# Finishing a gated recurrence tile by tile, making weights' low parts half a unit later, and loading an activation table earlier, in a three-mixer float32 transformer on one Trainium2 core

## The chip, the cores and the metric

The kernel runs on one core of one Trainium2 chip. The metric is the device time in microseconds of one execution, as the median of several runs; lower is better. Device time holds the span of the profile (first to last instruction) and a little around it.

## The reference, cut to what matters

The model takes 512 tokens of width 1024, kept in float32, through seven stages:

1. a gated FFN (SiLU gate, width 2816), a gated linear attention mixer, and another FFN;
2. an FFN, a differential attention mixer, and another FFN;
3. the third mixer, `hybrid_layer`, which ends the model.

The third mixer is what the change touches most. It projects the normalised input to six streams. Two of them, `xl` and `gl`, feed a recurrence, and four (`q`, `k`, `v`, `ga`) feed an attention of 8 heads:

```python
    xl = causal_depthwise_conv(xl, conv_w, conv_b)
    # rg_lru:
    r = sigmoid(xg @ w_a + b_a);  i = sigmoid(xg @ w_i + b_i)
    log_a = -LRU_C * r * softplus(-lam)
    a = exp(log_a)
    mult = sqrt(-expm1(2.0 * log_a));  mult[first token] = 1.0
    bterm = mult * (i * xb)
    h[t] = a[t] * h[t-1] + bterm[t]        # along the 512 tokens
    y_lru = h * silu(gl)
    y_att = attention(rms(q), rms(k), v) * silu(ga)
    out = x + gate * (concat(y_lru, y_att) @ w_out)
```

Every stage begins with an RMS norm, so it needs `rsqrt(mean(x*x) + eps)`, which this kernel makes from a logarithm and an exponential.

## The kernel before, in words

**Layout and matmuls.** All activations are held transposed, as tiles of 128 channels x 512 tokens. Every large matmul is made with float32 precision out of three faster ones: weights and activations are each split into a high part (`whi`, `xh`) and a low part (`wlo`, `xl`), and `rows` (line 1606) adds hi x hi, hi x lo and lo x hi. The weights come in panels (SyncE's queue loads them into four `raw` buffers, line 579) that are cut into units of 128 output channels. A unit is 8 x 3 = 24 matmuls of 512 columns. Unit numbers below are written as n; a unit's parts live in one of NSLOT = 4 slots, so unit n + 3's parts can be made once TensorE is done with unit n - 1.

**Who makes the parts.** ScalarE makes `whi` of a unit by a copy (`w_hi`, line 614), VectorE makes `wlo` as `raw - whi` (`w_lo`, line 1029) and waits for `whi`. SyncE may refill a `raw` buffer when VectorE has made the last `wlo` of its panel (`lo_done`, in `load`, line 575).

**Order of work.** Each engine runs its instructions in program order and waits on semaphores. For the mixers the order is a list of steps, written by hand for differential attention (`diff_steps`, line 182) and by a planner with due times for the third mixer (`hybrid_steps`, line 262). All engines walk the same list. A unit is issued as two steps, `("half", tag, i, 0)` and `("half", tag, i, 1)`, each 12 matmuls, and other steps stand between: `attend n` (scores of query block n, its row maximum on VectorE, its exponential on ScalarE), `comb n` (VectorE divides by the sum), `turn n` (TensorE transposes the block, ScalarE copies it out of PSUM), `pv`, `vT`, `ss` (sum of squares for the norm of q or k), `qk` (that norm applied on VectorE, ScalarE copies k's halves), `gmm`/`gadd` (gates of the recurrence), `lru p` (piece p of the recurrence), and the gate and output steps. A due time counts half-steps: `(15, ("lru", 5))` puts piece 5 beside the 15th half.

In the third mixer the units follow as xl0 to xl3, q0, k0, v0, q1, gate 4, k1, v1, q2, k2, v2, gate 0, q3, k3, v3, and five more gates. The block `attend 0` stands before the first half of k1. Around the change the list of before reads:

```
half q1 0, lru 1, qk k0, vT 0, half q1 1, done q1, lru 2, half gate4 0, lru 3, ss q1, half gate4 1, done gate4, qk q1,
attend 0, half k1 0, gmin 4, attend 1, comb 0, gexp 4, half k1 1, done k1, lru 4, gate 4,
attend 2, comb 1, half v1 0, ss k1, turn 0, attend 3, comb 2, half v1 1, done v1, lru 5, qk k1, turn 1,
attend 4, comb 3, half q2 0, vT 1, turn 2, attend 5, comb 4, half q2 1, done q2, lru 6, turn 3,
attend 6, comb 5, half k2 0, ss q2, pv 0, turn 4, attend 7, comb 6, half k2 1, done k2, qk q2, turn 5,
attend 8, comb 7, half v2 0, ss k2, turn 6, attend 9, comb 8, half v2 1, done v2, qk k2, turn 7,
attend 10, comb 9, half gate0 0, vT 2, pv 1, ya 0, ...
```

**When TensorE waits in it.** `attend n` needs the row maximum of `attend n-2` (two PSUM banks). `turn n` needs `comb n` and ScalarE's copy of `turn n-1` (one bank). `ss` needs ScalarE's square of that projection. A unit's first half needs the bank of the unit three before to have been read.

**The recurrence** (lines 973 to 1000 on ScalarE, 1519 to 1543 on VectorE). Its four tiles of channels stand side by side in `rg` (the decay a), `ig` (i * xb), `th` (the square root) and `xc` (the convolution's result, then h). Pieces 0 to 3 make a and the argument of the square root. Piece 4 on ScalarE is one exponential over 2048 columns (the square root as exp of half a logarithm). Piece 5 on VectorE is one memset for the first token, one multiplication over 2048 columns and the scans of tiles 0 and 1, piece 6 the scans of tiles 2 and 3.

**Tables.** ScalarE's functions lie in tables. `act` (line 596) loads the one with logarithm and exponential at the first Exp or Ln after a Silu, Sigmoid or Tanh (line 599); the loads in the other direction are put in by the compiler and show under line 604. In an FFN the last Silu comes at the last gate tile of part 1; the next Ln is that of the following stage's norm (`norm_factor`, line 637). In the third mixer TensorE can't begin before this norm is done; in the differential one the first sum of squares of k waits for it.

## Time and profile before

| | us |
|---|---|
| median of 3 runs | 2320.44 (2319.05 to 2321.05) |
| the profiled execution | 2316.55 |
| its span | 2314.8 |
| TensorE busy | 2252.8 (97%) |
| VectorE busy | 1270.2 (55%) |
| ScalarE busy | 907.0 (39%) |
| GpSimd busy | 154.0 (7%) |
| mean granted clock of TensorE | 0.992 |

The profiled execution took 3.9 us less than the median; its span lies 1.75 us under its own time. Busy time is the time in which an engine has an instruction under way; idle time of an engine that isn't on the path to the end costs nothing. "PEclk" is the clock that TensorE was granted: 1.00 is 2.4 GHz, 0.50 is 1.2 GHz.

### The profile page before, as it was taken

How to read it: one execution, taken by the hardware profiler on the slowest of the kernel's cores; microseconds unless marked ns; L12 is line 12 of the kernel's file. 1: busy time of each engine (PE TensorE's matmuls, PEld its weight loads, DVE VectorE, ACT ScalarE, POOL GpSimd, SP SyncE). 2: the span in 40 equal slices, each digit the busy share in tenths (PEclk: the TensorE clock that was granted, in tenths of full speed). 3: DMA queues.
4: the chain of work that ended last, by engine and by line, in shares of the span. 5: the costliest groups of instructions: out<-in, count | busy, mean ns of one | idle time of the engine just before them, and what ended most of it. 6: DMA issues, size and time to landing. Idle time of an engine off the chain costs nothing.

```text
span 2314.8 us, 24688 instructions
## 1 busy us (share of the span) xinstructions
PE 2252.8 (97%) x9842; PEld 1798.7 (78%) x9842; DVE 1270.2 (55%) x1964; ACT 907.0 (39%) x1399; POOL 154.0 (7%) x127
## 2 busy tenths in 40 slices
PE   7999999899899999999999999999999999999999
PEld 6888887676677888888888887777688888876677
DVE  6443445877755434454433446777566536546663
ACT  4222223555433222233322325777442222237562
POOL 2000012000040000020000021000220000110000
PEclk9999999999999999999999999999999999999999
DMA  5323224021124232133223223222144334232210
GB/s 186 101 82 109 96 69 148 19 92 55 37 75 157 86 123 91 64 118 109 86 97 109 78 87 107 71 71 89 55 136 146 118 118 141 87 114 64 74 55 37
DMA packets 201747, 217.39 MB, mean 94 GB/s; under 512 B 4969, under 2 KB 194537, under 8 KB 201633
## 3 DMA queue, kind: packets, MB, share of 16 engines
q1 hardware_dynamic: 194960, 193.48, 25.8%
q0 software_dynamic: 6528, 22.26, 2.8%
q8 instruction: 79, 1.29, 0.2%
q14 instruction: 36, 0.29, 0.0%
q10 hardware_dynamic: 144, 0.08, 0.0%
HBM read 213.66 MB, written 6.32 MB: 95 GB/s over the span
## 4 chain that ended last, share of the span: by engine, by line
PE 88%; DVE 7%; ACT 3%; issue 2%; DMA 0%; SPq 0%; DVEq 0%; ACTq 0%
PE ps L1573 86%; PE ps L1577 1%; DVE sb_wlo L1037 1%; ACT sb_whi L604 1%; DVE sb_gla_at L1289 1%; DVE sb_gla_ek L1274 1%; DMA sb_raw<-ffn_w_gu 0%; ACT sb_xh L604 0%; DVE sb_gla_eq L1277 0%; DVE sb_xl L1042 0%; DVE sb_gla_xb L1269 0%; ACT sb_hyb_rg L604 0%; DVE sb_dif_p L1344 0%; DVE sb_gla_d L1256 0%; ACT sb_dif_k L604 0%
## 5 line engine op out<-in xcount | busy, mean ns | idle before, releaser
L1573 PE MATMUL ps<-sb_xh,sb_whi 128*128 128x512 f32 x2120 | 849.0, 400 | 24.0 <-DVE sb_xl L1042 10.1
L1573 PE MATMUL ps<-sb_xh,sb_wlo 128*128 128x512 f32 x2120 | 831.3, 392 | 0.0
L1573 PE MATMUL ps<-sb_xl,sb_whi 128*128 128x512 f32 x2120 | 830.9, 392 | 0.0
L1037 DVE TENSOR_TENSOR sb_wlo<-sb_raw,sb_whi 128x1024 fp32r<-128x1024 f32 (+2 forms) x401 | 475.1, 1189 | 554.6 <-ACT sb_whi L604 553.3
L604 ACT ACTIVATE sb_whi<-sb_raw 128x1024 fp32r<-128x1024 f32 (+2 forms) x401 | 387.1, 968 | 601.2 <-PE ps L1573 592.9
L1573 PEld LDWEIGHTS ps<-sb_xh,sb_whi 128*128 128x128 f32 x2120 | 402.1, 190 | 118.8 <-issue 26.4
L1573 PEld LDWEIGHTS ps<-sb_xl,sb_whi 128*128 128x128 f32 x2120 | 401.8, 190 | 86.9 <-issue 6.0
L1573 PEld LDWEIGHTS ps<-sb_xh,sb_wlo 128*128 128x128 f32 x2120 | 401.1, 189 | 86.0
L1573 PE MATMUL ps<-sb_ffn_ah,sb_whi 128*128 128x512 f32 x704 | 277.6, 394 | 0.0
L1573 PE MATMUL ps<-sb_ffn_ah,sb_wlo 128*128 128x512 f32 x704 | 276.0, 392 | 0.0
L1573 PE MATMUL ps<-sb_ffn_al,sb_whi 128*128 128x512 f32 x704 | 273.3, 388 | 0.0
L1066 DVE TENSOR_TENSOR sb_ffn_u<-ps,sb_rb 128x512 f32<-128x512 f32 x88 | 60.7, 690 | 179.1 <-PE ps L1573 179.1
L1573 PEld LDWEIGHTS ps<-sb_ffn_ah,sb_wlo 128*128 128x128 f32 x704 | 132.1, 188 | 30.9
L1573 PEld LDWEIGHTS ps<-sb_ffn_al,sb_whi 128*128 128x128 f32 x704 | 132.2, 188 | 29.4
L604 ACT ACTIVATE sb_ffn_ah<-sb_ffn_u 128x512 fp32r<-128x512 f32 x88 | 55.6, 632 | 252.1 <-DVE sb_ffn_u L1072 252.1
L1573 PEld LDWEIGHTS ps<-sb_ffn_ah,sb_whi 128*128 128x128 f32 x704 | 132.4, 188 | 26.3
L604 ACT ACTIVATE sb_ffn_g<-sb_ffn_g 128x512 f32<-128x512 f32 x88 | 55.6, 632 | 167.4 <-DVE sb_ffn_g L1063 167.3
L1075 DVE TENSOR_TENSOR sb_ffn_al<-sb_ffn_u,sb_ffn_ah 128x512 fp32r<-128x512 f32 x88 | 61.0, 693 | 61.4 <-ACT sb_ffn_ah L604 61.4
L2012 POOL TENSOR_TENSOR sb_sqs<-sb_xT 128x512 f32<-128x512 f32 x7 | 9.2, 1311 | 1254.9 <-DVE sb_xT L1101 900.5
L1063 DVE TENSOR_TENSOR sb_ffn_g<-ps,sb_rb 128x512 f32<-128x512 f32 x88 | 60.2, 684 | 25.2 <-ACT sb_rb L604 25.2
L2018 POOL TENSOR_TENSOR sb_sqs<-sb_sqs,sb_sq 128x512 f32<-128x512 f32 x44 | 71.8, 1632 | 3.4
L1072 DVE TENSOR_TENSOR sb_ffn_u<-sb_ffn_u,sb_ffn_g 128x512 f32<-128x512 f32 x88 | 60.9, 692 | 11.1 <-ACT sb_ffn_g L604 2.4
(249 smaller groups left out, 1774.6 us busy)
## 6 DMA issues: line engine op xcount, KB each, us to landing
sb_raw<-ffn_w_gu SPq DMA_DIRECT2D x86, 1024.0 KB, 5.2
sb_raw<-ffn_w_down SPq DMA_DIRECT2D x32, 1024.0 KB, 4.9
sb_raw<-gla_w_in SPq DMA_DIRECT2D x12, 1024.0 KB, 5.4
sb_raw<-diff_w_in SPq DMA_DIRECT2D x12, 1024.0 KB, 5.2
sb_ada_raw<-w_ada POOLq DMA_DIRECT2D x12, 1024.0 KB, 6.3
sb_raw<-w_in SPq DMA_DIRECT2D x10, 1024.0 KB, 5.2
sb_raw<-ffn_w_down SPq DMA_DIRECT2D x16, 512.0 KB, 3.5
sb_raw<-ffn_w_down SPq DMA_DIRECT2D x16, 256.0 KB, 2.7
```

What stands on the lines that cost most here:

```text
L604: return e.activation(out, in_, func, bias=bias, scale=scale)
L1037: e.tensor_tensor(lo, raw[panel % NRAW][:, 0:nk, off:off + 128], hi.bitcast(F32), ALU.subtract).then_inc(sem["w_lo"], 1)
L1063: e.tensor_tensor(g[:, :], psum[FFN_RING[p % 6]][:, :], rb[:, :], ALU.mult).then_inc(sem["f_g"], 1)
L1066: e.tensor_tensor(v[:, :], psum[FFN_RING[(p + 1) % 6]][:, :], rb[:, :], ALU.mult).then_inc(sem["f_u"], 1)
L1072: e.tensor_tensor(v[:, :], v[:, :], g[:, :], ALU.mult).then_inc(sem["f_p"], 1)
L1075: e.tensor_tensor(al[:, j, :], v[:, :], ah[:, j, :].bitcast(F32), ALU.subtract).then_inc(sem["f_al"], 1)
L1274: e.tensor_tensor(K[:, :], K[:, :], ks[h % 2][:, :], ALU.mult).then_inc(sem["g_mk"], 1)
L1289: e.copy_predicated(diag, m, psum[GLA_RING[ring[0] % 3]][:, :].rearrange("p (n c) -> p n c", c=128)).then_inc(sem["g_at"], 1)
L1573: return e.matmul(out, lhsT, rhs, start=start, stop=stop, skip_group_check=skip)
L1577: ins = e.transpose(psum[bank][:, c * 128:(c + 1) * 128], src[:, c * 128:(c + 1) * 128], ident)
L2012: e.tensor_tensor(sqs[:, :], x[:, 0, :], x[:, 0, :], ALU.mult).then_inc(sem["sq"], 1)
L2018: e.tensor_tensor(sqs[:, :], sqs[:, :], sq[:, :], ALU.add).then_inc(sem["sq"], 1)
```

## The change

It makes three edits.

1. **Recurrence tile by tile.** ScalarE's exponential over 2048 columns becomes four over 512, as pieces 4 to 7, and VectorE's memset, multiplication and scan come tile by tile, as pieces 5 to 8. Two pieces are new in the list: `lru 7` stands between `done k2` and `qk q2`, `lru 8` between `done v2` and `qk k2`. Pieces 4, 5 and 6 keep their places (their due times change by 0.4, which moves nothing).
2. **Low parts at the second half.** In the differential and the third mixer VectorE calls `w_lo` at a unit's second half and no longer at its first. ScalarE's `w_hi` stays where it was.
3. **Table during the FFN.** ScalarE loads the table of logarithm and exponential once the last gate tile of each FFN's part 1 is done, before its down projection, and not at the norm that follows.

```diff
--- before.py
+++ after.py
@@ -310,8 +310,8 @@
 
     for tag, i in units[:3]:
         done(tag, i, -1)
-    due.extend([(3.6, ("lru", 0)), (7.6, ("lru", 1)), (9, ("lru", 2)), (10, ("lru", 3)), (13, ("lru", 4)),
-                (15, ("lru", 5)), (17, ("lru", 6))])
+    due.extend([(3.6, ("lru", 0)), (7.6, ("lru", 1)), (9, ("lru", 2)), (10, ("lru", 3)), (12.6, ("lru", 4)),
+                (14.6, ("lru", 5)), (16.6, ("lru", 6)), (18.6, ("lru", 7)), (20.6, ("lru", 8))])
     halves = [("half", tag, i, k) for tag, i in units[3:] for k in range(2)]
     for h in halves[:12]:
         beside(h)
@@ -593,11 +593,14 @@
             w = Waits(e)
             table = ["ln_exp"]
 
+            def ln_exp_table():
+                if table[0] != "ln_exp":
+                    e.preload_act_table_set("natural_log_exp_and_others")
+                table[0] = "ln_exp"
+
             def act(out, in_, func, scale=1.0, bias=0.0, accum=None):
                 if func in (ACT.Exp, ACT.Ln):
-                    if table[0] != "ln_exp":
-                        e.preload_act_table_set("natural_log_exp_and_others")
-                    table[0] = "ln_exp"
+                    ln_exp_table()
                 elif func in (ACT.Silu, ACT.Sigmoid, ACT.Tanh, ACT.Sqrt):
                     table[0] = func
                 if accum is None:
@@ -652,6 +655,8 @@
                         act(gb[j % 2][:, :], gb[j % 2][:, :], ACT.Silu).then_inc(sem["f_silu"], 1)
                         w.wait_ge(sem["f_p"], J + 1)
                         act(ah[:, j, :], ub[j % 2][:, :], ACT.Copy).then_inc(sem["f_ah"], 1)
+                    if part:
+                        ln_exp_table()
                     for m in range(KT):
                         w_hi(u)
                         w_hi(u + 1)
@@ -995,9 +1000,10 @@
                         act(lru_ln[t], th[:, t, :], ACT.Ln, bias=col("one")).then_inc(sem["h_ln"], 1)
                         w.wait_ge(sem["h_ln"], 2 * t + 1)
                         act(th[:, t, :], th[:, t, :], ACT.Ln, scale=2.0, bias=small[:, 49:50]).then_inc(sem["h_ln"], 1)
-                elif piece == 4:
-                    w.wait_ge(sem["h_m"], 4)
-                    act(th[:, :, :], th[:, :, :], ACT.Exp, scale=0.5).then_inc(sem["h_sqrt"], 1)
+                elif piece < 8:
+                    t = piece - 4
+                    w.wait_ge(sem["h_m"], t + 1)
+                    act(th[:, t, :], th[:, t, :], ACT.Exp, scale=0.5).then_inc(sem["h_sqrt"], 1)
 
             e.dma_start(par[:, :], a["par"]).then_inc(sem["par"], 16)
             e.preload_act_table_set("natural_log_exp_and_others")
@@ -1297,8 +1303,8 @@
                     if s[0] == "half":
                         _, tag, h, half = s
                         if not half:
-                            w_lo(u)
                             continue
+                        w_lo(u)
                         u += 1
                         b = psum[DIF_IN[d_unit[tag, h] % 2]]
                         used(w, u - 1)
@@ -1430,7 +1436,7 @@
                         w_lo(u)
                         u += 3
                     elif s[0] == "half":
-                        if s[3] == 0:
+                        if s[3] == 1:
                             w_lo(u)
                         u += s[3]
                     elif s[0] == "done" and s[1] == "xl":
@@ -1525,20 +1531,15 @@
                     for t in (2 * piece - 6, 2 * piece - 5):
                         w.wait_ge(sem["h_ln"], 2 * t + 2)
                         e.tensor_tensor(th[:, t, :], th[:, t, :], lru_ln[t], ALU.subtract).then_inc(sem["h_m"], 1)
-                elif piece == 5:
-                    w.wait_ge(sem["h_sqrt"], 1)
-                    e.memset(th[:, :, 0:1], 1.0).then_inc(sem["h_one"], 1)
-                    w.wait_ge(sem["h_one"], 1)
+                elif piece > 4:
+                    t = piece - 5
+                    w.wait_ge(sem["h_sqrt"], t + 1)
+                    e.memset(th[:, t, 0:1], 1.0).then_inc(sem["h_one"], 1)
+                    w.wait_ge(sem["h_one"], t + 1)
                     w.wait_ge(sem["h_ix"], 1)
-                    e.tensor_tensor(ig[:, :, :], ig[:, :, :], th[:, :, :], ALU.mult).then_inc(sem["h_b"], 1)
-                    scans(0)
-                elif piece == 6:
-                    scans(2)
-
-            def scans(t0):
-                w.wait_ge(sem["h_a"], 4)
-                w.wait_ge(sem["h_b"], 1)
-                for t in (t0, t0 + 1):
+                    e.tensor_tensor(ig[:, t, :], ig[:, t, :], th[:, t, :], ALU.mult).then_inc(sem["h_b"], 1)
+                    w.wait_ge(sem["h_a"], 4)
+                    w.wait_ge(sem["h_b"], t + 1)
                     e.tensor_tensor_scan(xc[:, t, :], rg[:, t, :], ig[:, t, :], 0.0, ALU.mult,
                                          ALU.add).then_inc(sem["h_scan"], 1)
```

## Rows read from the trace of the kernel before

**Rows 1.** Engines by stretch: busy us (count) of PE, PEld, DVE, ACT, POOL; granted clock.
```profile
1693.00:2054.00 361.00, 361.00 (x1610) 298.49 (x1610) 196.35 (x302) 101.51 (x127) 26.20 (x25) 1.00 0.39 129
2054.00:2150.00 96.00, 85.39 (x332) 62.52 (x330) 58.84 (x89) 60.91 (x85) 1.16 (x2) 0.95 0.20 63
```

**Rows 2.** TensorE in order of time, third mixer: start, us; idle before it in brackets.
```profile
2134.45 0.44 PE L1573 MATMUL ps<-sb_hyb_k,sb_hyb_q 128*128 128x384 f32 x1 [0.94 <-DVE sb_hyb_st L1494]
...
2139.85 1.68 PE L1573 MATMUL ps<-sb_hyb_sq,sb_cst 128*128 128x512 f32 x2 [2.04 <-ACT sb_hyb_sq L604]
...
2153.85 0.84 PE L1577 MATMUL ps<-sb_cst,sb_sqs 128*128 128x128 f32 x3 [4.29 <-ACT sb_hyb_pt L604]
```

**Rows 3.** ScalarE in order of time, start of the differential mixer.
```profile
1408.76 1.28 ACT L599 ACT_TABLE_LOAD   x1 [3.02 <-PE ps L1573]
...
1412.23 0.63 ACT L604 ACTIVATE sb_dif_sq<-sb_dif_qb 128x512 f32<-128x512 f32 x1 [0.82 <-DVE sb_dif_qb L1313]
```

**Rows 4.** TensorE in order of time, start of the differential mixer.
```profile
1413.01 1.10 PE L1573 MATMUL ps<-sb_dif_sq,sb_cst 128*128 128x512 f32 x2 [1.54 <-ACT sb_dif_sq L604]
```

**Rows 5.** All engines in order of time, start of the third mixer.
```profile
2058.47 1.28 ACT L599 ACT_TABLE_LOAD   x1 [1.21 <-PE ps L1573]
...
2060.48 0.63 ACT L604 ACTIVATE sb_rb<-sb_lnb 128x512 f32<-128x512 f32 x1
...
2063.58 0.76 PE L1573 MATMUL ps<-sb_xh,sb_whi 128*128 128x512 f32 x1 [5.14 <-DVE sb_xl L1425]
```

**Rows 6.** VectorE's waits in the third mixer: us in all, times, longest.
```profile
DVE sb_wlo L1037 <- ACT sb_whi L604: 50.3, 22, 7.7
```

**Rows 7.** VectorE in order of time, third mixer, q1 to k1.
```profile
2116.76 1.23 DVE L1037 TENSOR_TENSOR sb_wlo<-sb_raw,sb_whi 128x1024 fp32r<-128x1024 f32 x1
...
2134.09 0.29 DVE L1494 CUSTOM_DVE_ANT_0 sb_hyb_p<-ps,sb_hyb_causal 128x128 f32<-128x128 f32 x1
...
2135.91 1.23 DVE L1037 TENSOR_TENSOR sb_wlo<-sb_raw,sb_whi 128x1024 fp32r<-128x1024 f32 x1 [1.51 <-ACT sb_whi L604]
...
2137.65 0.42 DVE L1494 CUSTOM_DVE_ANT_0 sb_hyb_p<-ps,sb_hyb_causal 128x256 f32<-128x256 f32 x1
```

**Rows 8.** ScalarE in order of time, third mixer.
```profile
2139.14 0.57 ACT L604 ACTIVATE sb_hyb_sq<-ps 128x512 f32<-128x512 f32 x1
2139.71 1.91 ACT L604 ACTIVATE sb_hyb_th<-sb_hyb_th 128x2048 f32<-128x2048 f32 x1
...
2153.34 0.36 ACT L604 ACTIVATE sb_hyb_pt<-ps 128x256 f32<-128x256 f32 x1
```

**Rows 9.** The chain that ended last, third mixer: start, us.
```profile
2146.69 2.30 DVE sb_hyb_ig L1533
...
2149.08 2.34 DVE sb_hyb_xc L1542 x2
```

**Rows 10.** VectorE's instructions by shape, third mixer: busy, mean ns.
```profile
L1527 DVE TENSOR_TENSOR sb_hyb_th<-sb_hyb_th,sb_hyb_pt 128x512 f32<-128x512 f32 x3 | 2.0, 684 | 0.0
```

**Rows 11.** Engines by stretch, after a wait of TensorE.
```profile
1413.00:1415.00 2.00, 1.99 (x7) 1.34 (x8) 1.16 (x1) 1.64 (x3) 0.00 (x0) 1.00 0.00 0
...
2139.80:2143.70 3.90, 3.85 (x9) 2.43 (x10) 1.88 (x6) 3.90 (x5) 0.00 (x0) 0.56 0.00 0
2153.80:2157.50 3.70, 3.65 (x12) 3.16 (x13) 2.72 (x7) 2.30 (x5) 0.00 (x0) 0.54 0.00 0
```

**Rows 12.** VectorE in order of time, third mixer, k2 and v2.
```profile
2166.44 0.69 DVE L1494 CUSTOM_DVE_ANT_0 sb_hyb_p<-ps,sb_hyb_causal 128x512 f32<-128x512 f32 x1 [2.58 <-PE ps L1573]
...
2176.57 0.69 DVE L1451 COPY sb_hyb_vt<-ps 128x512 f32<-128x512 f32 x1 [1.92 <-PE ps L1573]
```

**Rows 13.** TensorE in order of time, third mixer, turn 7 and pv 1.
```profile
2176.38 0.60 PE L1577 MATMUL ps<-sb_cst,sb_hyb_p 128*128 128x128 f32 x4
...
2180.44 2.37 PE L1573 MATMUL ps<-sb_hyb_pt,sb_hyb_v 128*64 128x512 f32 x8
```

**Rows 14.** ScalarE in order of time, third mixer, copy of turn 7.
```profile
2179.20 0.58 ACT L604 ACTIVATE sb_hyb_pt<-ps 128x512 f32<-128x512 f32 x1
```

## The prediction, made before the changed kernel was run

> **What bounds the kernel now.** I read the stretches first. The FFN before the third mixer shows TensorE busy for 361.00 of 361.00 us: nothing that is made quicker elsewhere can shorten such a stretch. The first 96 us of the third mixer show 85.39 busy of 96.00, at a mean granted clock of 0.95 [rows 1]. So the change can win only where TensorE stands still or runs slowly, and that is at the starts of the mixers and in the third mixer's first 100 us. The second view is TensorE in order of time with the idle time before each instruction. In the third mixer it waits 5.14 us for the norm [rows 5], then 0.94 us before the scores of block 2, 2.04 us before the sum of squares of k1 and 4.29 us before turn 2 [rows 2]. In the differential mixer it waits 1.54 us at its start [rows 4]. The third view is the chain of waits behind each of these, which tells what is late. The last is the clock after them: after 1.54 us of standing still it is 1.00, after 2.04 and after 4.29 us it is 0.56 and 0.54 for nearly four microseconds [rows 11], so a removed wait gives back more than its own length.
>
> **The table load.** It takes 1.28 us and stands at the start of both mixers between TensorE's sum and the logarithm [rows 3, 5]. In the third mixer everything runs in series here (load, logarithm, exponential 0.63, then the normalised tiles, then the first matmul), so all 1.28 us come off the wait of 5.14. In the differential mixer TensorE waits 1.54 us for the square of k0, which waits for the same load [rows 3, 4]: again 1.28, and 0.26 stays. The load itself goes to a place where ScalarE has slack and TensorE is covered by weights made ahead: the FFN stretch is 100% TensorE with ScalarE at 101.51 of 361.00 [rows 1], so I cost it at nothing; without that cover it would cost its 1.28 each time. The loads that follow FFNs 0 and 1 end no wait that I list, so they are worth nothing. Term: **2 x 1.28 = 2.6 us**, bounds 0 (if the wait is taken over by something else) and 2.8 (1.54 + 1.28).
>
> The trace shows the logarithm 0.01 us behind the end of the load (2058.47 + 1.28 = 2059.75, the exponential then at 2060.48 [rows 5]). The Trainium skill, page "ScalarE: Activation LUTs", section "What ACT_TABLE_LOAD costs", counts a drain of about 1.38 us on top of each load. I go by the row; by the page the third mixer's wait would shrink by 2.66 and the differential one would vanish, an estimate of 4.2 us for this term.
>
> **The low parts.** At a first half VectorE waits for ScalarE's high part, which waits for TensorE to be through with the unit before: 50.3 us in 22 waits in the third mixer [rows 6]. Most cost nothing, since VectorE is only 55% busy. Two matter.
> - At q1, `w_lo` (1.23 us at 2116.76) stands ahead of a multiplication and of the norm of k0 [rows 7]. Behind them, everything up to the first `attend` comes up to 1.2 us sooner: ScalarE's k0 copies, the logarithms, the norm of q1 and the row maximum of block 0, which comes at 2134.09. TensorE's scores of block 2 wait for that maximum [rows 2]. Of the 0.94 us I take 0.8 off.
> - At k1, the row maximum of block 1 is ready to be taken at about 2134.5, but VectorE first waits 1.51 us for the high part and takes 1.23 us for the low one, then the gate's minimum, and reaches it at 2137.65 [rows 7]. ScalarE's exponential of block 1 waits for it, and behind that exponential stands the square of k1 at 2139.14 [rows 8], for which TensorE waits 2.04 us [rows 2]. With `w_lo` moved past both, block 1 comes 2.7 us sooner plus the 1.1 of the point above. ScalarE then makes the high part, the exponential, the gate's exponential and the square without a gap, and ends at about 2136.7, when TensorE has just ended v1's first half. I leave 0.2 us: 1.8 off.
>
> Behind the moved `w_lo` stand SyncE's refills. They come half a unit later, 2.7 us and what stands between, and load for units that are several ahead, so I cost them at nothing (rival 3 says when not). Term: **2.6 us**, bounds 0 and 3.0 (0.94 + 2.04).
>
> **The scans.** Between the copy of v1 and the norm of k1 VectorE does a memset, a multiplication of 2.30 and two scans of 2.34 together, 4.8 us from 2146.6 [rows 9]. The norm of k1, ScalarE's two copies of k1 and the copy of turn 1 at 2153.34 stand behind it [rows 8], and turn 2 waits 4.29 us for that copy [rows 2]. The piece of one tile is a multiplication of 0.69 (as the subtraction of that shape, 684 ns [rows 10]), a scan of 1.17 (half of 2.34) and 0.15 for the memset: 2.0 us, 2.8 less. That leaves 4.29 - 2.8 = 1.5. ScalarE's exponential before it shrinks too, from 1.91 [rows 8] to about 0.6, but a new tightness comes: since TensorE arrives sooner, turn 1 already waits a little for ScalarE's copy of turn 0, which stands behind an exponential, a high part and the norm of k1. I put both together at 1.8 us. Term: 4.29 - 1.8 = **2.5 us**, bounds 1.3 (the copy of turn 0 costing 1.2 more) and 4.3.
>
> **The clock.** After the wait of 2.04 us, 3.9 us ran at 0.56, and after that of 4.29, 3.7 us at 0.54 [rows 11]: 3.9 x 0.44 + 3.7 x 0.46 = 3.4 us lost. The waits that remain (0.2, then about 0.8 and 1.0) are each shorter than the 1.54 us that left the clock at 1.00. Term: **3.4 us**, bounds 0 and 3.4. The 5.14 us at the start become 3.9, still near the 4.29 that halved the clock, and I take nothing there. The Trainium skill, page "TensorE: Matmul & The Clock Gate", section "What's actually happening", says that the number of slow matmuls at one and the same place differs from run to run. By it this term would keep its size in the mean and scatter; no single trace shows that.
>
> **What is given back.** Pieces `lru 7` and `lru 8` are new in k2 and v2, 2.0 us each on VectorE. Between block 7's maximum at 2166.44 and the copy of v2 at 2176.57 VectorE is idle for 1.92 us just ahead of that copy [rows 12], and the change adds 2.0 and the low part of k2 (1.23): the copy comes up to 1.3 late. I take 0.4, since one of the waits for high parts [rows 6] falls in here too. Then `lru 8` stands ahead of the norm of k2, whose k copies stand ahead of the copy of turn 7 on ScalarE, which ended at 2179.20 + 0.58 = 2179.8 [rows 14]. It will end at 2179.8 + 0.4 + 2.0 = 2182.2 at the least, while `pv 1` wants it at 2180.44, one unit half after turn 7 at 2176.38 [rows 13]. Part of this shows already at turn 7. Term: **-1.9 us**, bounds 0 and -5 (both waits in full with their slow clock). `lru 6`, now 2.0 instead of 2.34, changes nothing.
>
> **Sum.** 2.6 + 2.6 + 2.5 + 3.4 - 1.9 = 9.2 us. From the profiled execution, 2316.55 (span 2314.8 and 1.75 around it), that makes 2307.4. The runs shown have a median 3.9 us above it, 2320.44, and against that I forecast **2311.2 us**. A measurement of this kernel can tell about 0.2%, 4.6 us, from no change.
>
> **The rivals.**
> 1. *Waits stay, and with them the slow clock.* The remaining 1.8 us and the new 1.9 us each fall in one piece and halve the clock as the 2.04 us did: another 3.4 us. For it: they are close to that wait in length. Against: each is made of two waits with matmuls between. 9.2 - 3.4 = 5.8: 2314.6. Chance 0.14.
> 2. *What is won early is only lost at the next turn.* The softmax chain (maximum, exponential, division, transpose, copy) sets the pace, TensorE arrives sooner and waits as much. Only the table loads and the 0.8 us stay: 3.4, 2317.0. Against it: VectorE spends 50.3 us of this mixer waiting for high parts, which wait for TensorE [rows 6], so the chain has room. Chance 0.13.
> 3. *Slower: low parts too late for TensorE.* The low part of unit n + 3 now waits behind two blocks of attention. It decides once it ends later than two units after the first half of n, some 11 us (48 matmuls at 361.00/1610 us, 0.22 each [rows 1]). Then each of the 15 units from k1 on would wait about one low part: 15 x 1.23 = 18.5, less 9.2: 9.3 slower, 2329.7. Against it: the delay is about 4 us. Chance 0.04.
> 4. *A table switch costs its drain too.* ScalarE would then save 2.66 us at each start, of which the differential mixer can use 1.54: 1.6 more, 2309.6. That is the page's rule above; the row speaks against it. Chance 0.03.
> 5. *The load doesn't move.* The compiler puts in a second load at the norm, since copies lie between the early one and the logarithm. Then 2.6 us are missing: 2313.8. Chance 0.04.
>
> **How the numbers follow.** My own sum has 0.62. The lower end takes the give-back as 0 and the wait at turn 2 as gone, and 1 us of the slow clock at the start: 9.2 + 1.9 + 1.8 + 1.0 = 13.9, 2306.5. The upper end takes in rival 2: 2317.0. Outside lie rival 3 and tails of the first two cases, together about 0.15. Faster by over 0.2% (below 2315.8) are my sum nearly whole (0.61), rival 1 mostly (0.12) and rivals 4 and 5: 0.80. Within 0.2% are rival 2 and the rest: 0.16. Slower: 0.04.
>
> **What would show it.** A table load in each FFN's part 1, none at the norms; idle 3.9 us before the third mixer's first matmul and 0.3 before the differential mixer's sum of squares. No wait near 2 us before the sum of squares of k1; at most 1.8 us before turns 1 and 2 together, and the clock at 1.00 behind them. New waits of 1 to 2 us around turn 7 and `pv 1`. I am wrong if turn 1 or turn 2 still waits over 2 us, if the clock drops behind turn 7, or if TensorE waits for a low part.

## The result, and the profile after

| | before | after |
|---|---|---|
| median, us | 2320.64 (2319.05 to 2321.05, 4 runs) | 2307.26 (2306.07 to 2308.53, 4 runs) |
| ratio of the times | | 0.9944, 95% interval 0.9926 to 0.9961 |
| the profiled execution, its span | 2316.55, 2314.8 | 2308.53, 2306.7 |
| TensorE, VectorE, ScalarE busy | 2252.8, 1270.2, 907.0 | 2252.1, 1270.6, 906.2 |
| mean granted clock | 0.992 | 0.992 |

The changed kernel is 13.4 us faster by these medians. The forecast was 9.2 us and 2311.2 us, in a range of 2306.5 to 2317.0. TensorE's busy time and mean clock are the same in both profiles, so what went between these two is idle time. Slow clock went too, behind k1 and turn 2, but the profile after has more of it in the linear attention (last section). Two later sets of runs gave the same pair 10.9 us (2319.59 to 2308.66) and 10.6 us (2319.01 to 2308.39) apart.

TensorE in order of time in the profile after: start, us, form, and the idle time before it in brackets. These are its waits that answer to [rows 2, 4, 5, 13], with their neighbours.

```profile
1416.65 1.10 PE L1574 MATMUL ps<-sb_dif_sq,sb_cst 128*128 128x512 f32 x2 [0.26 <-ACT sb_dif_sq L607]
...
2065.01 0.77 PE L1574 MATMUL ps<-sb_xh,sb_whi 128*128 128x512 f32 x1 [3.85 <-DVE sb_xl L1431]
...
2133.76 0.44 PE L1574 MATMUL ps<-sb_hyb_k,sb_hyb_q 128*128 128x384 f32 x1 [0.38 <-DVE sb_hyb_st L1500]
...
2141.96 0.41 PE L1578 MATMUL ps<-sb_cst,sb_hyb_p 128*128 128x128 f32 x2 [0.66 <-ACT sb_hyb_pt L607]
...
2146.73 0.52 PE L1578 MATMUL ps<-sb_cst,sb_sqs 128*128 128x128 f32 x3 [0.95 <-ACT sb_hyb_pt L607]
...
2168.75 0.63 PE L1578 MATMUL ps<-sb_cst,sb_hyb_p 128*128 128x128 f32 x4 [0.83 <-ACT sb_hyb_pt L607]
...
2173.40 2.37 PE L1574 MATMUL ps<-sb_hyb_pt,sb_hyb_v 128*64 128x512 f32 x8 [0.47 <-ACT sb_hyb_pt L607]
```

The reader is to see: 1.54 became 0.26 at the differential mixer's start, 5.14 became 3.85 at the third mixer's start, both 1.28 or 1.29 less. Block 2's 0.94 became 0.38. The sum of squares of k1 waits no more (2.04 before). Turn 2's 4.29 became 0.95, and turn 1 waits 0.66, which it didn't before. The last two lines, turn 7 and `pv 1`, are new waits, 1.30 us together.

The loads of the table in the profile after, all of its line:

```profile
L598 ACT ACT_TABLE_LOAD  x11: 1283/1283/1283, 325.9 to 2111.4; - x11
```

Four of the eleven have moved. They stand at 325.9, 993.1, 1354.6 and 2003.5, each right behind the last gate tile of an FFN's part 1; in the profile before they stood at the norms at 383.6, 1063.6, 1408.8 and 2058.5. The last of them:

```profile
2003.54 1.28 ACT L598 ACT_TABLE_LOAD   x1
```

The other seven are where they were, three of them right ahead of the logarithm of a norm that no FFN comes just before (646.2, 1713.7 and 2111.4). ScalarE around the third mixer's norm, where [rows 5] had the load at 2058.47, goes straight from its wait to the logarithm:

```profile
2061.19 0.69 ACT L607 ACTIVATE sb_lnb<-ps,sb_par 128x512 f32<-128x512 f32 x1 [1.22 <-PE ps L1574]
2061.91 0.63 ACT L607 ACTIVATE sb_rb<-sb_lnb 128x512 f32<-128x512 f32 x1
```

VectorE around k1 and v1 in the profile after, against [rows 7, 9]:

```profile
2133.41 0.29 DVE L1500 CUSTOM_DVE_ANT_0 sb_hyb_p<-ps,sb_hyb_causal 128x128 f32<-128x128 f32 x1
...
2134.23 0.41 DVE L1500 CUSTOM_DVE_ANT_0 sb_hyb_p<-ps,sb_hyb_causal 128x256 f32<-128x256 f32 x1
...
2135.22 1.23 DVE L1043 TENSOR_TENSOR sb_wlo<-sb_raw,sb_whi 128x1024 fp32r<-128x1024 f32 x1 [0.17 <-ACT sb_whi L607]
...
2142.34 0.69 DVE L1540 TENSOR_TENSOR sb_hyb_ig<-sb_hyb_ig,sb_hyb_th 128x512 f32<-128x512 f32 x1
2143.13 1.23 DVE L1543 TENSOR_TENSOR_SCAN sb_hyb_xc<-sb_hyb_rg,sb_hyb_ig 128x512 f32<-128x512 f32 x1
2144.27 0.73 DVE L1463 SCALAR_TENSOR_TENSOR sb_hyb_rq<-ps,sb_par,sb_hyb_rq 128x512 f32<-128x512 f32 x1
```

Block 1's row maximum follows block 0's by 0.82 us and stands ahead of the low part; in [rows 7] 3.56 us and the low part lay between them. Ahead of the norm of k1 stand one multiplication and one scan of 1.23, together 2.0 us with the memset, where [rows 9] had 4.8.

### The profile page after: what moved, and what is told of

It is laid out like the page before. It is cut to its first block, busy times and chain, and to the rows that moved or that the text cites. A ratio compares the mean times of both kernels' runs of the same rounds, so it can differ in the third digit from the quotient of the medians.

```text
span 2306.7 us, 24697 instructions
## 1 busy us (share of the span) xinstructions
PE 2252.1 (98%) x9842; PEld 1799.0 (78%) x9842; DVE 1270.6 (55%) x1970; ACT 906.2 (39%) x1402; POOL 154.0 (7%) x127
## 3 DMA queue, kind: packets, MB, share of 16 engines
q8 instruction: 79, 1.29, 0.2%
## 4 chain that ended last, share of the span: by engine, by line
PE 89%; DVE 6%; ACT 3%; issue 2%; DMA 0%; SPq 0%; DVEq 0%; ACTq 0%
PE ps L1574 88%; PE ps L1578 1%; DVE sb_wlo L1043 1%; ACT sb_whi L607 1%; DVE sb_gla_ek L1280 0%; DVE sb_gla_at L1295 0%; DMA sb_raw<-ffn_w_gu 0%; ACT sb_xh L607 0%; DVE sb_xl L1048 0%; DVE sb_gla_eq L1283 0%; DVE sb_gla_xb L1275 0%; DVE sb_gla_d L1262 0%; ACT sb_hyb_th L607 0%; DVE sb_gla_on L1206 0%; ACT sb_gla_z L607 0%
```

## How the runs are compared

An execution's time scatters: the 27 of the kernel before that ran beside e1 lie between 2316.01 and 2323.75 us, and the slower ones show the lower mean clock (0.992 for the first of these two, 0.987 for the second). TensorE came to the differential mixer anywhere between 1411.5 and 1418.4 us in the fourteen profiles. So beside each median I take lengths of stretches between fixed points of TensorE. From each row named, its idle time is taken off for the arrival: the differential mixer from its first sum of squares to the wait for the low part of its output (in the profile before 1413.01 less 1.54, to 1618.32 less 1.97), then up to the sum for the third mixer's norm, then to the start of turn 2, then to the wait of 0.5 us for a low part in the last projection, and the whole from the first point to the end of the span.

| kernel | differential | to third mixer | to turn 2 | to projection | whole |
|---|---|---|---|---|---|
| before | 204.88 | 440.33 | 97.17 | 134.56 | 903.33 |
| e6, low parts in the differential mixer only | 203.95 | 439.30 | 97.16 | 134.45 | 900.82 |
| e1, table only | 203.56 | 439.38 | 94.46 | 134.20 | 897.54 |
| e3, recurrence only | 204.84 | 439.54 | 92.59 | 134.45 | 897.34 |
| e2, low parts only | 203.93 | 439.42 | 92.90 | 133.91 | 896.13 |
| f9, low parts and recurrence | 203.96 | 439.31 | 89.66 | 134.08 | 893.37 |
| after | 202.68 | 440.31 | 87.35 | 134.05 | 890.31 |
| e4, f12: after, again | 202.68, 202.70 | 439.34, 439.34 | 88.79, 88.87 | 134.08, 134.08 | 890.88, 891.32 |
| e9, f11: pieces moved | 202.69, 202.69 | 439.90, 440.10 | 86.54, 86.52 | 132.30, 132.27 | 887.43, 887.50 |

The differential column repeats to 0.04 us for one and the same code of that mixer. The second column, whose code differs only by the place of one table load, takes values 1 us apart, with and without that edit. In "to turn 2" there is a similar chance of some 1.5 us: from the third mixer's first matmul to the norm of q0 it is 47.58 us in the profile after, 49.03 and 49.05 in its repeats, 48.58 in that of before (the wait for that norm not counted).

## The experiments

**e1, the table alone.** The kernel before with the third edit: `ln_exp_table()` is called after the last gate tile of each FFN's part 1 (the call alone, cut).

```diff
+                    if part:
+                        ln_exp_table()
                     for m in range(KT):
```

> Only the table edit is made. My theory (each wait of TensorE shrinks by what is taken off its own chain): the wait before the differential mixer's first sum of squares goes from 1.54 to 0.26 us and that before the third mixer's first matmul from 5.14 to 3.9, the waits at k1 (2.04) and at turn 2 (4.29) stay. 2.5 us faster, and up to 1 us more from a shorter stretch at half clock behind the third mixer's start. Rival (the load is only moved onto another chain, or the compiler puts in a second one): 0 us, with a load still at the norm or TensorE waiting inside an FFN.

Measured: 2315.87 us against 2319.59 (11 and 27 runs), ratio 0.9981 (0.9972 to 0.9990), 3.7 us. TensorE in order of time in e1:

```profile
2065.72 0.76 PE L1578 MATMUL ps<-sb_xh,sb_whi 128*128 128x512 f32 x1 [3.86 <-DVE sb_xl L1430]
...
2135.62 0.44 PE L1578 MATMUL ps<-sb_hyb_k,sb_hyb_q 128*128 128x384 f32 x1 [0.98 <-DVE sb_hyb_st L1499]
...
2141.03 1.10 PE L1578 MATMUL ps<-sb_hyb_sq,sb_cst 128*128 128x512 f32 x2 [2.04 <-ACT sb_hyb_sq L607]
...
2145.89 0.41 PE L1582 MATMUL ps<-sb_cst,sb_hyb_p 128*128 128x128 f32 x2 [0.45 <-ACT sb_hyb_pt L607]
...
2154.56 0.88 PE L1582 MATMUL ps<-sb_cst,sb_sqs 128*128 128x128 f32 x3 [4.87 <-ACT sb_hyb_pt L607]
```

The wait at the start lost its 1.28 us, and the 2.04 us at k1 stayed. The differential column is 1.32 shorter. The third mixer gained 2.71 up to turn 2, more than its 1.28. Of the rest, 0.97 is the chance named above (47.60 us from the first matmul to the norm of q0, against 48.58), and 0.46 lies between block 2 and turn 2 (18.94 against 19.40). There the clock did not fall behind the 2.04 us (below), which saved 1.49 us of matmul time; but TensorE came to the turns earlier and waited 0.45 and 4.87 us, 1.03 more than before, and so most of it was taken back.

**e2, the low parts alone.** The kernel before with `w_lo(u)` at the second half in both mixers. The third mixer's half of it:

```diff
-                        if s[3] == 0:
+                        if s[3] == 1:
                             w_lo(u)
```

> Only the low parts are made at the second half. My theory: the waits of 0.94 and 2.04 us before the scores of block 2 and the sum of squares of k1 fall to about 0.4 and 0, the half clock behind the latter goes (1.7 us), the wait of 4.29 at turn 2 stays: 4 to 5.5 us faster. Rival (what is won early is lost at the next turn): turns 1 and 2 together wait 6 us or more, the whole under 1.5 us faster.

Measured: 2314.91 us, ratio 0.9973 (0.9963 to 0.9982), 4.7 us. In the list of TensorE's waits the one at k1 is gone, turn 1 has a new one and turn 2 keeps most of its own:

```profile
2145.99 0.41 PE L1577 MATMUL ps<-sb_cst,sb_hyb_p 128*128 128x128 f32 x2 [1.39 <-ACT sb_hyb_pt L604]
...
2153.52 0.52 PE L1577 MATMUL ps<-sb_cst,sb_sqs 128*128 128x128 f32 x3 [3.73 <-ACT sb_hyb_pt L604]
```

The two turns wait 5.12 us together; I had expected 4.29, and the rival 6 or more. A wait of 0.52 us that the profile before has at 2246.52, ahead of a late `pv`, is gone as well; it is there in e1, e3 and e6 and in no kernel with this edit in the third mixer. Turn 1's 1.39 us is the tightness of ScalarE's copy of turn 0 that my scan term spoke of. On ScalarE it stands here behind the exponential over 2048 columns:

```profile
2140.98 1.92 ACT L604 ACTIVATE sb_hyb_th<-sb_hyb_th 128x2048 f32<-128x2048 f32 x1 [1.00 <-DVE sb_hyb_th L1527]
...
2145.58 0.26 ACT L604 ACTIVATE sb_hyb_pt<-ps 128x128 f32<-128x128 f32 x1
```

In the changed kernel, with the short one, turn 1 waits 0.66.

**e3, the recurrence alone.** The kernel before with pieces 4 to 8 tile by tile; VectorE's part of it, cut:

```diff
-                    e.tensor_tensor(ig[:, :, :], ig[:, :, :], th[:, :, :], ALU.mult).then_inc(sem["h_b"], 1)
-                    scans(0)
+                    e.tensor_tensor(ig[:, t, :], ig[:, t, :], th[:, t, :], ALU.mult).then_inc(sem["h_b"], 1)
```

> Only the recurrence goes tile by tile. My theory: the wait at turn 2 goes from 4.29 to about 1.5 us and its half clock goes (1.7 us), the wait of 2.04 at k1 stays with its half clock, new waits of about 1 us come around turn 7 and pv 1: 3 to 4 us faster. Rival (the softmax chain sets the pace): the wait at turn 2 stays above 3 us, and the new waits make it 0 to 1 us slower.

Measured: 2315.47 us, ratio 0.9986 (0.9977 to 0.9995), 4.1 us by the medians and 3.2 by the ratio. TensorE's waits:

```profile
2142.99 1.10 PE L1569 MATMUL ps<-sb_hyb_sq,sb_cst 128*128 128x512 f32 x2 [2.04 <-ACT sb_hyb_sq L604]
...
2153.03 0.52 PE L1573 MATMUL ps<-sb_cst,sb_sqs 128*128 128x128 f32 x3 [1.96 <-ACT sb_hyb_pt L604]
...
2179.50 2.37 PE L1569 MATMUL ps<-sb_hyb_pt,sb_hyb_v 128*64 128x512 f32 x8 [1.31 <-ACT sb_hyb_pt L604]
```

Turn 2's wait fell from 4.29 to 1.96, where I had expected about 1.5, and `pv 1` gave back 1.31. The half clock behind k1, which I had expected to stay, did not come (1.00, as in e1). So the fair pair for the two turns is e1, with 0.45 and 4.87 us: 3.36 us less. ScalarE's shorter exponential and VectorE's shorter pieces are both in it; e8 tells them apart.

**e4, all three again, beside these.**

> The changed kernel once more, beside the three single edits on the same chip. If the edits add up, it is faster by the sum of the three, 10 to 13 us; if two of them clear the same wait, by clearly less than the sum. Against the first comparison (13.4 us of medians, of which the two profiled executions show 8.1): if the linear attention stage's clock is chance, the executions of this one scatter by 2 to 5 us and that stage's length with them.

Measured: 2308.66 us, ratio 0.9949 (0.9936 to 0.9962), 10.9 us; the waits are those of the profile after, within 0.03 us. The three single edits sum to 12.5 us, 1.6 more than all three together. Each of these gains is known to some 2 or 3 us only, so the times show no more than that nothing very large is counted twice. The stretch from the norm of q0 to the projection's wait tells more: 176.25 us before, 171.53 with the low parts, 172.19 with the recurrence, 168.26 with both (f9). The parts sum to 8.8 us and both give 8.0.

**e6, the low parts in the differential mixer only.** The profile before had a wait of 0.42 us there that I had costed at nothing.

```diff
                         if not half:
-                            w_lo(u)
                             continue
+                        w_lo(u)
```

> The kernel before with one edit: in the differential mixer alone, VectorE makes a unit's low part at its second half; everything else as before. The pair of edits for both mixers gave 4.7 us, and took TensorE's wait of 0.42 us in the differential mixer away. Theory (what is gained there is that one wait): that wait goes, all of the third mixer stays as in before (2.04 us before the sum of squares of k1, 4.29 before turn 2), and the time is 0 to 1 us below the kernel before, ratio 0.9996 to 1.0. Rival (the differential mixer gains a good part of the 4.7 us, by more than its waits show): 2 us or more, ratio 0.9991 or below.

The wait is this one, in the profile before:

```profile
1453.16 0.50 PE L1573 MATMUL ps<-sb_dif_k,sb_dif_q 128*128 128x512 f32 x1 [0.42 <-DVE sb_dif_st L1344]
```

Measured: 2317.85 us against 2318.71 (12 and 23 runs), ratio 0.9995 (0.9986 to 1.0004), 0.9 us, not to be told from nothing by time. The differential stretch tells it: 203.95 against 204.88, and every pair of kernels with and without this edit differs there by 0.86 to 0.95. So the theory held in size, but the gain is twice the one wait of 0.42; where the other half lies I did not follow up.

**f9, low parts and recurrence without the table.**

> The changed kernel without its third edit: the table of logarithm and exponential is loaded at the norms again, low parts at the second half and the recurrence tile by tile stay. Theory (the parts add up: the table is worth its 1.28 us at each of the two mixers' starts and touches nothing else): TensorE waits 1.54 us at the differential mixer's start and 5.14 at the third mixer's, the waits before turns 1 and 2 stay at 0.66 and 0.95 us, and the stretch from TensorE's arrival at the differential mixer to the end is 2.6 us longer than in the changed kernel, about 893. Rival (the third mixer's start is tied to what follows, as the softmax chain lags by as much as TensorE is early): turns 1 and 2 wait less by about as much as the start waits more, and the stretch is within 1.5 us of the changed kernel's 890.3 to 890.9.

Measured: 2311.29 us, ratio 0.9964 (0.9951 to 0.9977); the changed kernel beside it 2308.39, 2.9 us less.

```profile
2066.32 0.76 PE L1569 MATMUL ps<-sb_xh,sb_whi 128*128 128x512 f32 x1 [5.14 <-DVE sb_xl L1426]
...
2144.30 0.41 PE L1573 MATMUL ps<-sb_cst,sb_hyb_p 128*128 128x128 f32 x2 [0.67 <-ACT sb_hyb_pt L604]
...
2149.06 0.52 PE L1573 MATMUL ps<-sb_cst,sb_sqs 128*128 128x128 f32 x3 [0.92 <-ACT sb_hyb_pt L604]
```

Both turns wait as in the changed kernel (0.66 and 0.95), though the mixer began 1.28 us later. The start doesn't trade with the softmax chain: what the table gives is kept whole. The rival, which is my rival 2 for this part, falls. The whole stretch, 893.37, is 2.05 to 3.06 us above the three profiles of the changed kernel.

**e8, ScalarE's exponential whole again.** The changed kernel with one exponential over 2048 columns in piece 4.

```diff
-                elif piece < 8:
-                    t = piece - 4
-                    w.wait_ge(sem["h_m"], t + 1)
-                    act(th[:, t, :], th[:, t, :], ACT.Exp, scale=0.5).then_inc(sem["h_sqrt"], 1)
+                elif piece == 4:
+                    w.wait_ge(sem["h_m"], 4)
+                    act(th[:, :, :], th[:, :, :], ACT.Exp, scale=0.5).then_inc(sem["h_sqrt"], 4)
```

> The changed kernel, but ScalarE's exponential of the recurrence is again one over 2048 columns (1.91 us), and VectorE's multiplications and scans stay tile by tile. Theory (VectorE's scans, not ScalarE's exponential, made the wait before turn 2): ScalarE had 1.56 us of idle time behind the short exponential in the changed kernel, but the long one must also wait for the last subtraction at 2137.6, so it ends at about 2139.5, 0.75 us after the row maximum of block 2 is there. Turn 1 or turn 2 waits 0.5 to 0.8 us more, and nothing else changes: 0.5 to 1 us above the changed kernel. Rival (the split of the exponential carries the gain): turn 2 waits 3 us or more again and the clock halves behind it, 3 to 5 us above the changed kernel.

Measured: 2307.17 us (5 runs), ratio 0.9952 (0.9939 to 0.9965), no different in time from the changed kernel. TensorE in e8:

```profile
2140.63 0.41 PE L1577 MATMUL ps<-sb_cst,sb_hyb_p 128*128 128x128 f32 x2 [1.46 <-ACT sb_hyb_pt L607]
...
2145.46 0.52 PE L1577 MATMUL ps<-sb_cst,sb_sqs 128*128 128x128 f32 x3 [0.98 <-ACT sb_hyb_pt L607]
```

Turn 1 waits 0.80 us more than in the changed kernel, turn 2 0.03 more, and the stretch to turn 2 is 0.8 us longer than in the repeats (89.63 against 88.79 and 88.87). e2, with the long exponential and VectorE's long pieces, has 5.12 us at the two turns; here it is 2.44. (e2 lacks the table edit, but f9 shows that the turns don't feel it.) So of the first edit's gain 2.7 us are VectorE's, where I had worked out 2.8, and splitting the exponential carries 0.8.

**e7 and f10, how late the low parts may come.** The changed kernel with the low parts two units later still, and one unit later.

```diff
-                        w_lo(u)
+                        w_lo(u - 2)
```

(in both mixers; f10 has `u - 1`.)

> The changed kernel, but in both mixers the low part is made two whole units later still, at the second half of the unit but two behind, so that VectorE makes the low part of unit n + 1 about one unit ahead of TensorE and not three. This asks how far away the edge is that my rival 3 was about. Theory (three units of lead are far more than is needed; about 11 us of it are spare): no wait of TensorE for a low part, the time within 2 us of the changed kernel. Rival (low parts come too late once VectorE has attention work ahead of them): TensorE waits for sb_wlo once in most of the 15 units from k1 on, 1.2 us or more each and with a slower clock behind, 10 us or more above the changed kernel.

Measured: 2318.16 us, ratio to before 0.9997 (0.9988 to 1.0005): the whole gain is gone. Neither theory: TensorE waits for a low part twice and no more in the two mixers' units, in e7 at

```profile
1449.19 0.47 PE L1574 MATMUL ps<-sb_xh,sb_whi 128*128 128x512 f32 x1 [0.96 <-DVE sb_wlo L1043]
...
2129.11 0.52 PE L1574 MATMUL ps<-sb_xh,sb_whi 128*128 128x512 f32 x1 [2.80 <-DVE sb_wlo L1043]
2129.42 0.63 PE L1574 MATMUL ps<-sb_xl,sb_whi 128*128 128x512 f32 x1
```

and behind the second one the granted clock is 0.54 (2129.1 to 2132.8 us), which the 0.63 us of the last row show too. VectorE made that low part only at 2127.73, behind the norm of k0. At the differential mixer's end the low part of the attention's output (`sb_xl`, not a weight) came late too: a wait of 1.94 us, none in the changed kernel, and a clock of 0.68 in the 4 us behind it. The whole stretch is 900.18, some 9 us more than in e4 and f12: 1.2 in the differential column, 3.8 up to the third mixer, 3.8 from there to turn 2.

> The changed kernel with the low parts of both mixers one whole unit later (two units later had cost TensorE waits of 0.96 us in the differential mixer and of 2.80 us in the third, the latter at the first unit for which VectorE still had a norm ahead). Theory (the lead of three units that the changed kernel leaves has one unit and more to spare): no wait for sb_wlo in either mixer, the stretch from the arrival at the differential mixer to the end within 1.5 us of the changed kernel's 890.3 to 890.9. Rival (the placement of the changed kernel is at its edge): at least one wait of 1 us for sb_wlo, and 2 us or more in the stretch.

Measured: 2309.80 us beside 2308.39, the whole stretch 891.58: no wait for a low part in either mixer, as the theory has it. One wait at the differential mixer's projection is new:

```profile
1633.39 0.50 PE L1574 MATMUL ps<-sb_xh,sb_whi 128*128 128x512 f32 x1 [1.15 <-DVE sb_xl L1364]
```

VectorE makes two weights' low parts in one go ahead of it (2.36 us at 1626.25), where the changed kernel makes one (1.23). So the edge lies between one and two units beyond the change, and the first sign of it isn't a late weight but other work of VectorE's behind two low parts.

**e9 and f11, the new pieces moved off the path.** In the changed kernel piece 5 stands ahead of the norm of k1, 7 ahead of that of q2, 8 ahead of that of k2. What they make is used only at the output. ScalarE's exponentials of these pieces move along, as all engines walk the same list.

```diff
-                (14.6, ("lru", 5)), (16.6, ("lru", 6)), (18.6, ("lru", 7)), (20.6, ("lru", 8))])
+                (15.1, ("lru", 5)), (16.6, ("lru", 6)), (19.1, ("lru", 7)), (21.1, ("lru", 8))])
```

> The changed kernel with three pieces of the recurrence moved by two steps of VectorE's list: piece 5 from ahead of the norm of k1 to behind it and behind the row maximum that follows, piece 7 likewise behind the norm of q2, piece 8 behind the norm of k2. Theory (in the changed kernel these pieces of 2 us stand on the path to TensorE's waits of 0.95 us before turn 2, 0.83 before turn 7 and 0.47 before pv 1, while they themselves are due only at the output): the three waits shrink to 0.3 us or less each, 1.5 to 2.3 us below the changed kernel. Rival (the softmax chain sets the pace, so the wait only moves to the next turn): the sum of the waits between 2140 and 2180 us stays within 0.5 us of that of the changed kernel, 2.9 us, and so does the time.

Measured: 2306.36 us, ratio 0.9946 (0.9934 to 0.9957). On VectorE the norm of k1 now follows the copy of v1 at once:

```profile
2142.24 0.68 DVE L1457 COPY sb_hyb_vt<-ps 128x512 f32<-128x512 f32 x1
2142.84 0.74 DVE L1463 SCALAR_TENSOR_TENSOR sb_hyb_rq<-ps,sb_par,sb_hyb_rq 128x512 f32<-128x512 f32 x1
```

Between 2068 and 2279 us only the waits of 0.84, 0.32 and 0.38 for norms and for block 2, and this one are left:

```profile
2142.61 0.41 PE L1578 MATMUL ps<-sb_cst,sb_hyb_p 128*128 128x128 f32 x2 [0.67 <-ACT sb_hyb_pt L607]
```

> The kernel with pieces 5, 7 and 8 of the recurrence behind the norms of k1, q2 and k2 once more, beside the changed kernel on the same chip. Theory (the three waits that went, 2.25 us, are a gain of the kernel and not of one execution): the waits before turns 2 and 7 and before pv 1 are gone again, the stretch from TensorE's arrival at the differential mixer to the end is 887 to 889 us, against 890.3 to 890.9 for the changed kernel, and the median is 1 to 3 us lower. Rival (nothing is gained in the mean): the stretch is 890 us or more.

Measured: 2307.53 us beside 2308.39, ratio 0.9945 (0.9932 to 0.9957), the same waits gone, the whole stretch 887.50.

> The changed kernel a third time, as the measure for the others of this job. From the arrival at the differential mixer to the end 890 to 891.5 us, turn 2 waiting 0.9 us, turn 7 0.8, pv 1 0.5; the median within 1.5 us of 2308.

Measured: 2308.39 us, whole stretch 891.32, turns 1 and 2 0.65 and 0.92, turn 7 0.84, `pv 1` 0.46.

The waits before turns 2 and 7 and before `pv 1` went, 2.25 us, and came back nowhere. From the norm of q0 to the projection's wait the stretch is 165.36 and 165.32 us in e9 and f11, against 168.19, 168.22 and 168.26 in the three profiles of the changed kernel: 2.9 us, at a clock of 1.00 in all five. That is 0.6 more than the three waits; the rest shows as TensorE's busy time (163.1 us against 163.7 to 163.8). In time, the mean of the ten runs is 2306.2, that of the fourteen of the changed kernel 2307.8: 1.7 us, with standard errors of 0.6 and 0.5 us. So the gain is shown in the stretch; in time it is likely, and its size isn't settled (f11's median is 0.9 us under f12's, just short of what I expected).

## Why the prediction was right, and where it was off

**The table, 2.6 us: right.** 1.28 and 1.29 us came off the two waits. The loads in the FFNs cost nothing that shows. Take the stretch ahead of the third mixer: it has TensorE busy for 360.30 of 361.00 us (after) against 361.00, and the 0.70 is a wait for a norm's low parts at 1695.47 that the profile before has too (0.69 at 1692.78, just ahead of this window):

```profile
1693.00:2054.00 361.00, 360.30 (x1606) 297.57 (x1605) 196.89 (x305) 104.33 (x130) 26.36 (x25) 1.00 0.40 128
2054.00:2150.00 96.00, 88.35 (x361) 65.86 (x359) 64.19 (x104) 62.87 (x95) 1.16 (x2) 0.98 0.20 63
```

Rival 5 (the load stays) is out: eleven loads as before, and none is left at a norm that follows an FFN. One at a norm I overlooked: in the third mixer a load stands right ahead of the logarithm for q0, and TensorE waits 0.84 us for that logarithm.

```profile
2111.39 1.28 ACT L598 ACT_TABLE_LOAD   x1
2112.69 0.69 ACT L607 ACTIVATE sb_lnb<-ps,sb_par 128x512 f32<-128x512 f32 x1
```

Whether it could come earlier too was not tested. Rival 4 is out as well. With the drain of the page "ScalarE: Activation LUTs" of the Trainium skill, section "What ACT_TABLE_LOAD costs", the differential mixer's wait would have vanished; 0.26 us of it is left, as the row alone said.

**The low parts, 2.6 us: right in kind, too small.** Block 2's wait fell by 0.56 where I said 0.8, the sum of squares of k1 by 2.04 where I said 1.8. Three things were missing, as I had looked only at waits of 0.9 us and more. A wait of 0.24 us for the norm of k0, and what goes with it, went too: the stretch from the norm of q0 to block 2's scores, its wait included, shrank by 1.13 us. The wait of 0.52 us at 2246.52 went. And the step "two matter" left out the differential mixer: 0.93 us (e6).

**The scans, 2.5 us: right.** Turns 1 and 2 wait 0.66 + 0.95 = 1.61 us; the term had 1.8. Its reason holds in both parts: VectorE's share is 2.7 us (e2 against e8), and e2 and e8 show the copy of turn 0 behind ScalarE's long exponential (1.39 and 1.46 against 0.66).

**The clock, 3.4 us: right for the profile before, not for the kernel.** Behind turn 2 the clock is now 1.00. This is the profile after, at turns 1, 2, 7 and `pv 1`; columns as in [rows 11], the granted clock behind the five engines:

```profile
2141.90:2145.90 4.00, 3.81 (x20) 3.07 (x20) 3.78 (x7) 1.99 (x5) 0.00 (x0) 1.00 0.00 0
2146.70:2150.70 4.00, 3.97 (x22) 3.27 (x23) 3.67 (x12) 3.00 (x8) 0.00 (x0) 1.00 0.00 0
2168.70:2172.70 4.00, 3.95 (x22) 3.41 (x22) 3.82 (x8) 1.48 (x4) 0.00 (x0) 1.00 0.44 131
2173.40:2177.40 4.00, 4.00 (x16) 2.45 (x17) 2.27 (x9) 2.92 (x7) 0.00 (x0) 1.00 0.01 2
```

So rival 1 is out: four short waits, none with a slow clock. But the half that I counted behind k1's 2.04 us is there only sometimes. In e1, with the same wait in the same place, the windows behind it and behind turn 2 read

```profile
2141.00:2144.90 3.90, 3.87 (x16) 2.87 (x17) 1.88 (x6) 3.90 (x5) 0.00 (x0) 1.00 0.00 0
2154.50:2158.20 3.70, 3.64 (x13) 3.15 (x14) 2.72 (x7) 2.31 (x5) 0.00 (x0) 0.61 0.00 0
```

and in e3 it is 1.00 as well, while before and e6 have 0.56. From block 2 to turn 1, waits taken off, the four took 7.78, 7.62, 9.25 and 9.29 us: about 1.6 us, in two executions of four. Behind turn 2 the slow clock came each time that the wait was 3.7 us or longer (before, e1, e2, e6). The statement of the Trainium skill's page "TensorE: Matmul & The Clock Gate", section "What's actually happening", that the number of slow matmuls at a kernel's start differs from run to run, is of the same kind.

The two halves of the term aren't alike. Behind k1 a long wait follows, and it takes back most of what the clock gives: e1 and the profile before differ by 0.46 us from block 2 to turn 2, not by 1.5. So the clock term and the wait terms are right only together: where the clock holds, the waits to be won are larger. Behind turn 2 no such wait follows, and the half counts in full: from turn 2 to the projection e2 takes 133.91 us with a clock of 0.56 behind the turn, e9 132.30 with neither slow clock nor waits.

**The give-back, -1.9 us: right in place and size.** 0.83 at turn 7 and 0.47 at `pv 1`. When the pieces are moved (e9), the stretch behind turn 2 shrinks by 1.8 us. What I missed is that piece 5 itself, even of one tile, still stood on the path to turn 2.

**The sum.** Forecast 9.2. The table of stretches gives 12.0 to 13.0 us against the one profile of before (903.33 less 891.32, 890.88 and 890.31), some 1 us of it the chance in the second column or at the third mixer's start; the three pairs of medians give 13.4, 10.9 and 10.6. Part by part, the profiles before and after give 2.6 for the two norms (forecast 2.6), 0.9 in the differential mixer (0), 1.1 up to block 2 (0.8), 6.4 from there to turn 2 (1.8 + 2.5 + 1.7 = 6.0) and 0.5 behind it (1.7 of clock less 1.9 given back: -0.2). That makes 11.5, so I was short by 2.3 us.

That 2307.26 lies inside the range, 0.8 us above its lower end, is partly luck. I had built that end on three things: nothing given back, no wait left at turns 1 and 2, and less slow clock at the start. None of them came. The parts that I had missed and the scatter of the first set filled their place. Its 13.4 has some 2.5 us more than the other two sets; that is within the scatter of four runs, and no experiment separates it. Like for like, the spans of the two first profiles differ by 8.1 us and not by 13.0, because the changed kernel's came to the differential mixer 4.9 us later, with a slower clock on the way (last section).

**Rival 2 (lost at the next turn)** is out: turn 1 took 0.66 us back of the 5.9 that went at block 2, k1 and turn 2. **Rival 3 (low parts too late)** is out for this change, and e7 corrects its working: the edge lies nearly where I put it in distance (two units), but beyond it two late weights, one late output and the slow clock behind them cost about 10 us, not fifteen low parts. (The fifteen units are counted rightly: six gates follow v3 in the list, not five.)

## What to carry to other kernels

Read what stands ahead, on its own engine, of the instruction that the busiest engine waits for. Work that is needed late (a scan for the output, low parts for three units ahead) belongs behind it, and the place in the list is worth as much as the length: the same scans, moved behind a norm, gave another 2.9 us of the stretch. List the small waits as well, down to 0.2 us, in every stage that an edit touches; here they made up most of the shortfall. Count a slow clock behind a wait as a chance, not as a fixed price, unless several executions show it, and look whether a long wait behind it takes the time back.

## What the hardware showed that was not expected

The same wait of 2.04 us at the same instruction left TensorE at full clock in two executions and at 0.56 in two others. The clock differs over longer stretches too. In the linear attention, whose code is the same, the windows before

```profile
444.00:464.00 20.00, 18.20 (x67) 11.57 (x66) 12.66 (x24) 13.29 (x22) 0.00 (x0) 1.00 0.00 0
484.00:494.00 10.00, 9.45 (x53) 7.82 (x52) 9.90 (x22) 5.34 (x14) 0.00 (x0) 1.00 0.49 161
```

and after

```profile
444.00:464.00 20.00, 18.20 (x64) 12.75 (x63) 8.73 (x15) 12.36 (x19) 0.00 (x0) 0.83 0.00 0
484.00:494.00 10.00, 8.12 (x40) 6.96 (x39) 9.73 (x20) 3.52 (x8) 0.00 (x0) 0.83 0.34 106
```

show the granted clock at 1.00 and at 0.83. By the mixer's end (TensorE at 682.16 and 687.10 us) the two profiles are 4.9 us apart, 1.6 of them from ahead of it. Up to there the change has moved one table load, and no wait for a norm shows it; 4.9 us is more than half of what the change was forecast to bring. A shorter wait at the third mixer's start (3.85 for 5.14 us) didn't reliably shorten the slow stretch behind it: from the first matmul to the norm of q0 it is 47.6 to 49.1 us with the shorter wait and 48.0 to 48.6 with the longer. And a load of the table takes no more than its 1.28 us on ScalarE: in the profiles before and after, the instruction that follows begins 0.01 to 0.02 us behind it wherever it doesn't wait for another engine or a transfer.
